# Two feed-forwards in three parts, with the down products in the same list of pairs as the up products and three units of each down pair multiplied by the 7-product scheme

## The reference

```python
h = h + 0.5 * swiglu(rms_norm(h, ffn1_norm), ffn1_w_gate, ffn1_w_up, ffn1_w_down)
...                                  # attention, gated linear attention, merge, w_out
h = h + 0.5 * swiglu(rms_norm(h, ffn2_norm), ffn2_w_gate, ffn2_w_up, ffn2_w_down)
h = h + sigmoid(rms_norm(h, ple_norm) @ w_ple_gate) * (p @ w_ple_proj)
return rms_norm(h, final_norm)
# swiglu(x) = (silu(x @ w_gate) * (x @ w_up)) @ w_down, hidden width 5632
```

## Time and profile before

| | |
|---|---|
| median of 3 runs | 2217.74 us (2217.3 to 2218.07) |
| the profiled execution | 2217.39 us |
| its span, first to last instruction | 2215.3 us |
| PE busy | 2202.3 us, 99% of the span, 9899 matmuls and transposes |
| DVE busy | 1409.5 us, 64% |
| ACT busy | 1073.8 us, 48% |
| DMA | 425.68 MB, 192 GB/s mean |

### The profile page before, as it was taken

The page is one execution under the profiler, slowest core; times in us unless marked ns, Lnnn a source line. Parts: engine busy times, 40 slices in busy tenths (PEclk is TensorE's granted clock), DMA queues, the critical chain, the costliest instruction groups (busy, mean ns, idle before and its releaser), DMA issues.

```text
span 2215.3 us, 24399 instructions
## 1 busy us (share of the span) xinstructions
PE 2202.3 (99%) x9899; PEld 1817.2 (82%) x9899; DVE 1409.5 (64%) x1432; ACT 1073.8 (48%) x1183; POOL 39.4 (2%) x71
## 2 busy tenths in 40 slices
PE   9999999999999999999999999999999999999998
PEld 7888888888888888877777888888888888888886
DVE  5988645688755544445655665788864568875555
ACT  6545443454544444454444545464543346444454
POOL 0000000000010000010010000000000000000000
PEclk9999999999999999999999999999999999999999
DMA  8655555654555666655555665655546665556664
GB/s 288 239 176 193 179 190 186 233 214 173 190 179 187 200 193 195 180 174 169 175 170 161 186 186 180 232 205 180 201 171 190 190 237 200 186 182 198 190 190 143
DMA packets 165705, 425.68 MB, mean 192 GB/s; under 512 B 11592, under 2 KB 11600, under 8 KB 150368
## 3 DMA queue, kind: packets, MB, share of 16 engines
q1 hardware_dynamic: 163840, 419.21, 58.1%
q0 software_dynamic: 1472, 4.70, 0.8%
q10 hardware_dynamic: 288, 0.30, 0.0%
HBM read 422.06 MB, written 2.11 MB: 191 GB/s over the span
## 4 chain that ended last, share of the span: by engine, by line
PE 98%; DMA 1%; issue 0%; DVE 0%; ACT 0%; ACTq 0%; POOLq 0%; POOL 0%
PE acc L1493 18%; PE acc L1495 18%; PE acc L1494 18%; PE acc L1536 6%; PE acc L1538 6%; PE acc L1537 6%; PE turn L1538 4%; PE turn L1536 4%; PE turn L1537 4%; PE fox L1538 4%; PE fox L1537 4%; PE fox L1536 4%; PE turn L1513 1%; DMA raw<-in_ffn_up 0%; PE acc L1530 0%; PE turn L1787 0%
## 5 line engine op out<-in xcount | busy, mean ns | idle before, releaser
L1025 DVE TENSOR_TENSOR w_lo<-raw,w_hi 128x1024 fp32r<-128x1024 f32 x451 | 558.0, 1240 | 585.1 <-ACT w_hi L594 584.6
L594 ACT ACTIVATE w_hi<-raw 128x1024 fp32r<-128x1024 f32 x451 | 477.1, 1060 | 682.9 <-PE acc L1495 643.0
L1493 PE MATMUL acc<-w_hi,x_both 128*128 128x512 f32 x940 | 371.0, 395 | 0.8 <-DVE x_both L1188 0.8
L1495 PE MATMUL acc<-w_hi,x_both 128*128 128x512 f32 x940 | 366.6, 390 | 0.0
L1494 PE MATMUL acc<-w_lo,x_both 128*128 128x512 f32 x940 | 366.3, 390 | 0.0
L1493 PE MATMUL acc<-w_hi,slab_r 128*128 128x512 f32 x832 | 325.5, 391 | 0.0
L1495 PE MATMUL acc<-w_hi,slab_r 128*128 128x512 f32 x832 | 324.2, 390 | 0.0
L1494 PE MATMUL acc<-w_lo,slab_r 128*128 128x512 f32 x832 | 324.0, 389 | 0.0
L1493 PEld LDWEIGHTS acc<-w_hi,x_both 128*128 128x128 f32 x940 | 176.6, 188 | 42.5 <-issue 5.7
L1495 PEld LDWEIGHTS acc<-w_hi,x_both 128*128 128x128 f32 x940 | 176.5, 188 | 37.4
L1494 PEld LDWEIGHTS acc<-w_lo,x_both 128*128 128x128 f32 x940 | 176.7, 188 | 35.2
(11 more groups left out here) (432 smaller groups left out, 3513.6 us busy)
## 6 DMA issues: line engine op xcount, KB each, us to landing
raw<-in_ffn_w_down SPq DMA_DIRECT2D x176, 512.0 KB
raw<-in_ffn_up SPq DMA_DIRECT2D x50, 1024.0 KB, 4.9
raw<-in_w_in SPq DMA_DIRECT2D x96, 512.0 KB
lo_raw<-in_ffn_up SPq DMA_DIRECT2D x42, 1024.0 KB, 4.9
raw<-in_w_merge_gate SPq DMA_DIRECT2D x64, 512.0 KB
more<-in_ffn_up SPq DMA_DIRECT2D x25, 1024.0 KB, 4.9
raw<-in_ffn_up SPq DMA_DIRECT2D x33, 512.0 KB, 3.9
raw<-in_w_out SPq DMA_DIRECT2D x32, 512.0 KB
```

Of the source, the lines that this page charges most:

```text
L594: nc.scalar.activation(w_hi[:, slot, :, :], raw[:, slot, :, :], ACT.Copy).then_inc(hi_split, 1)
L1025: nc.vector.tensor_tensor(w_lo[:, slot, :, :], raw[:, slot, :, :], w_hi[:, slot, :, :].bitcast(F32), ALU.subtract).then_inc(lo_split, 1)
L1493: nc.tensor.matmul(to, hi(kt)[:, tok], w_hi[:, slot, k, :], start=kt == 0, stop=False)
L1495: last = nc.tensor.matmul(to, lo(kt)[:, tok], w_hi[:, slot, k, :], start=False, stop=kt == BK * nb - 1)
```

## The change

The two parts become three (16, 16 and 12 row tiles; 4, 4 and 3 up pairs). The down product of a part becomes two down pairs of 1024 columns each, with 8, 8 and 6 units of two row tiles. Up and down pairs stand in one list of 17 pairs for each ffn and alternate between the bank sets. Every pair but the first (in the first ffn the first two) has three units by the 7-product scheme, down pairs too. Input sums for the down pairs are made from the hidden values, three units for each part: unit 0 in the stage ahead of the part's last up stage, units 1 and 2 in the last up stage. B items are interleaved with S items; `turn_hidden` moves from behind the fifth item to behind the third on PE. The rows of h, p and the inputs of the last phases move to other rooms, and the thin weights of the projection are split later. The core of the diff:

```diff
-HALF_KT = (24, 20)
+PARTS = (4, 4, 3)
-US = 3
+US, HS = 3, 3
+def ffn_pairs():
+    pairs, j = [], 0
+    for part, ups in enumerate(PARTS):
+        kt0 = 4 * sum(PARTS[:part])
+        pairs += [Pair("up", part, j + n, UNITS, 4 * n) for n in range(ups)]
+        pairs += [Pair("down", part, n, 2 * ups, kt0) for n in range(2)]
+        j += ups
+    return pairs
-    own = [("S", pair, u) for u in range(UNITS)]
-    if pair > first:
-        own = [("B", pair, u) for u in range(US)] + own[US:]
-    if pair + 1 < pairs:
-        own = [*own[:-1], *[("A", pair + 1, u) for u in range(US)], own[-1]]
-    return own
+    b, a = shared_units(ffn, i), shared_units(ffn, i + 1)
+    plain = [("S", i, u) for u in range(b, PAIR[i].units)]
+    own = []
+    for u in range(b):
+        own.append(("B", i, u))
+        if len(plain) > 2:
+            own.append(plain.pop(0))
+    own += plain
+    if a:
+        behind = 2 if PAIR[i].units < UNITS else 1
+        own = [*own[:-behind], *[("A", i + 1, u) for u in range(a)], *own[-behind:]]
+    return own
+def turned_at(stage):
+    return 4 if len(stage) >= 10 else 3
```

More of the change, by code:

```diff
@@ L127, in item_tables @@
         slot, at, made = 0, b0, []
-        for p in range(first, pairs):
+        for i in range(first, PAIRS):
             stage = []
-            for kind, pair, u in stage_of(p, first, pairs):
+            for kind, pair, u in stage_of(name, i):
                 q = quads[at - b0]
@@ L164, in filled @@
         n = blk
-        for name in UPS:
-            if blk >= BLOCK[DOWN_OF[name]]:
-                n -= padded(up_items(name))
+        for name, later in NEXT_OF.items():
+            if blk >= BLOCK[later]:
+                n -= padded(ffn_items(name))
         return n // RING + 1
@@ L173, in split_after, with sum_number @@
         return AFTER[first][1][blk % RING // 2] if first in AFTER else blk - RING + 1
[L175 to L178, removed]
+    ADDED = {}
+    for name, first in FIRST.items():
+        for i in range(first, PAIRS):
+            if shared_units(name, i):
+                ADDED[name, i] = len(ADDED) + 1
+    ROWS = {"down1": GROUP["ffn1"] + 2 * (PAIRS - 2), "out": GROUP["out"], "down2": GROUP["ffn2"] + 2 * (PAIRS - 2)}
+    UP_TURN = {"ffn1": TURN["up1"], "ffn2": TURN["up2"]}
     def item_counts(name, it):
-        end = BLOCK[DOWN_OF[name]]
+        end = BLOCK[NEXT_OF[name]]
         return end - it.at if it is STAGES[name][-1][-1] else 1
+    def sum_number(name, pair, u):
+        first = (US + HS * len(PARTS)) * (name == "ffn2")
+        return first + u if PAIR[pair].kind == "up" else first + US + HS * PAIR[pair].part + u
     x_tm = x[0].rearrange("(t p) d -> p t d", p=P)
@@ L1413, in _ @@
                 else:
[L1414 removed]
+                    rows_out(c - 1, start, 1.0)
                 splits(start, 4, 6)
@@ L1538, in product, with plain_part, shared_products @@
                 return nc.tensor.matmul(to, x_rest, w, start=False, stop=stop, skip_group_check=primed)
-            def multiply_item(name, it, hi, lo, primed, last_unit, ready):
+            def plain_part(name, it, ct, hi, lo, primed):
+                banks, whole, rest = banks_of(name, it.pair), hi_quad(name, it.quad), lo_parts(name, it)[0]
+                for k in range(BK):
+                    for t in range(TT):
+                        tok, kt = slice(t * P, (t + 1) * P), BK * it.unit + k
+                        last = product(banks[2 * ct + t][:, :], hi(kt)[:, tok], lo(kt)[:, tok], whole[:, 2 * k + ct, :],
+                                       rest[:, 2 * k + ct, :], not primed and kt == 0,
+                                       not primed and kt == BK * PAIR[it.pair].units - 1, primed)
+                return last
+            def shared_products(name, it, hi, lo):
                 banks, whole = banks_of(name, it.pair), hi_quad(name, it.quad)
@@ L1562, in multiply_item @@
[L1562 to L1567 removed]
+                sum_hi, sum_lo = sums_of(it.pair, it.unit)
@@ L1569, in tiles_of, with feed_forward @@
+                for n, (x, x_rest, bank) in enumerate(of_tokens):
+                    last = product(banks[bank][:, :], x, x_rest, whole[:, n, :], rest[n], begin, end, it.kind == "B")
+                return last
             def tiles_of(first_turn):
                 return lambda j: pe.wait_ge(turned_lo, first_turn + j + 1)
-            def up_groups(name, hi, lo, sums=None, first_rows=None):
-                pairs, first = UPS[name]
+            hidden_of = of(slab_r, slab_r, 0, HID)
+            def feed_forward(name, x_pair, first_rows=None, p_turn=False):
+                down_turn = "down" + name[-1]
```

515 lines of the change are left out of this document (249 added, 266 removed).

## The result

The changed kernel takes 2238.26 us (median of 4 runs, 2238.05 to 2239.2) against 2217.52 (4 runs, 2217.14 to 2218.07) for the kernel before: ratio 1.0093, 95% interval 1.0079 to 1.0106. It is slower, as forecast, but by 20.7 us where I had said 7.5, and it lies above my range. Its profiled execution has a span of 2237.5 us, 22.2 more than before.

A forecast was written before the change was run, and what follows sets the result against it. PE's count of matmuls was taken to bound the kernel. Savings of 28.6 us against added waits of 11.4, 18.0 and 6.65 us gave +7.5 us, so 2225 us, with a range of 2209 to 2236.

The forecast's parts named there:

- twelve waits for the sums: Last up stage of each part and the stage ahead: input sums delay A1's split, 0.95 us each, 11.4 us.
- the long one of the short stage: First down stage of the last part: trio load, steps A1, then A0's split; PE stands still 5.9 us.
- the ones of the last stages: Last down stage: PE waits 2.65 us for splits; in the second ffn 0.9 and 3.1 us; sum 6.65 us.
- PE's 126 matmuls: Up and down pairs: 14 more pairs share units, saving 9 matmuls each at 0.227 us, 28.6 us off PE.
- the short stages: First down stage of each ffn's last part: waits ahead of B2, A0 and A1, 9.0 us per ffn, 18 us.
- the 2.1 us wait that I had forecast: Short down stage, ahead of A1: DVE gives an A each 4.86 us, PE takes 2.72, so PE waits 2.1 us.
- the first of my two figures: Short down stage: low clock for A0's 12 matmuls costs 0.6 us; through all three A items, 6.1 us a stage.
- the sum: Whole kernel: -28.6 + 11.4 + 18.0 + 6.65 = +7.5 us, 2225 us; other added work put at nothing.
- starts of both ffn: Beginning of each ffn: the prediction had no term for waits there, 0 us.
- Other stages lose their 1.7 us too: Rival: seven more stages that follow an up pair wait, 1.5 us each, giving 2235 us; chance 0.08.
- The price of a wait: Stages with input sums: a wait costs PE's idle until the split, 0.9 us, 0.95 with the handover.
- The wait of 5.9 us in the short stage is the first inside the kernel that could do this: Short down stage: the granted clock could fall to half behind this wait; rival with it low through A items, 2232, chance 0.15.

The follow-up runs named there:

- raw-space: Changed kernel with raw spaces 0, 1, 4, 0 for the second ffn's first four items, in place of 0, 1, 0, 1: 2235.03 us.
- plain-pair: Changed kernel with the last down pair of each ffn multiplied plainly, 9791 matmuls instead of 9773: 2230.05 us.
- The run with PE kept busy: Changed kernel with 75 matmuls whose results nobody reads filling PE's long waits: 2236.21 us.
- the short stage reordered: Changed kernel with the short down stage as B0 B1 B2 S3 S4 A0 A1 A2 S5: 2228.72 us.
- the sums moved: Changed kernel with ten of twelve input-sum places moved in DVE's and ACT's lists, out of the stretch ahead of the A items: 2224.44 us.
- The kernel of three edits: Changed kernel with each ffn's last down pair plain, raw spaces 0, 1, 4, 0 at the second ffn's start, and ten input sums moved: 2212.53 us.
- the list alone: Changed kernel with no down pair shared and no sums for them, raw and high-part spaces set at the starts: 2218.19 us.

## Why the prediction was right and wrong

**Right.** The sign, and the mechanism of every wait in three of the four groups: twelve waits for the sums (forecast 0.95 us, seen 0.95 to 0.99); the long one of the short stage (5.9; 5.62 and 5.41), through trio load, steps, then A0's split; the ones of the last stages (2.65 and 0.9; 2.67 and 0.98). The second ffn's was 2.72 and not 3.1. PE's 126 matmuls are 28.6 us as said. The clock fell behind both waits of the short stages (0.51 and 0.54 granted behind 5.62 and 5.41 us). By the rule of the Trainium skill that the prediction cites, "TensorE: Matmul & The Clock Gate", "Why this matters for your kernels", it should, and there the trace agrees. But it stayed low for A0 alone, where it took the place of the 2.1 us wait that I had forecast (2.4 and 2.0 us lost), the first of my two figures. That the short stages come to 18.1 us where I had said 18.0 is therefore luck in part: 4.2 us of forecast waits did not come, and 4.4 us of slow matmuls stood in their place.

**Wrong, in size**, by 13.9 us (21.4 accounted, 7.5 forecast). By the terms of the sum:

| term | forecast | measured |
|---|---|---|
| 126 matmuls | -28.6 | -28.6 |
| sums, 12 waits | +11.4 | 11.6 idle + 3.2 = +14.9 |
| short stages | +18.0 | 12.6 idle + 1.1 + 4.4 slow clock = +18.1 |
| last stages | +6.65 | 6.4 idle + 0.8 + 2.9 slow clock = +10.1 |
| starts of both ffn | 0 | 3.5 idle + 0.5 + 2.9 slow clock = +6.9 |

1. The step that failed most is "the sum", where other waits were put at nothing. Both starts were missing in it: the number of loads in a ffn sets which raw space the first ones get, and the change alters that number. None of my rivals had it ("Other stages lose their 1.7 us too" names others, and those did not wait). For the second ffn the raw-space and plain-pair runs show the cause, from both sides; for the first (0.68 us) it is read from the list and the trace alone.
2. The price of a wait. I priced PE's standing still at the time until the split is there, 0.95 with 0.05 for the handover. A stage with one takes 1.26 us longer, and over 21 waits the 0.27 that I left out are 5.7 us. The chain gave me the distance of matmul starts, and there was no wait in it from which to read that price; the earlier trace rows had three, and I did not measure around them.
3. The clock. "The wait of 5.9 us in the short stage is the first inside the kernel that could do this" was wrong: in the changed kernel it fell behind 2.80 and 2.72 us too, and there it came on top of the idle, 2.9 us each. The run with PE kept busy gave back all of it in the last stage and 1.6 us at the start. The earlier trace rows only showed that it falls some time after the last matmul.

## What to carry to other kernels

When an engine without slack is given less work, price each new wait at its idle plus what stopping and starting costs, and ask whether the clock falls behind it and what would hide that. When a change alters the number of items in a list, work out every rotation of buffers that counts from an end of it, at both ends. And work saved on PE by added work on DVE is worth its place in DVE's list: the same 126 matmuls cost 21 us or bring 9, by where sums, B items and loads stand.

## What was not expected of the hardware

Over eleven kernels with waits of PE, behind the first 25 us: matmuls started 0.43 us apart behind each of the twelve waits of 3.5 us and longer, at once or up to five matmuls later (behind the 3.78 us of the plain pair the first four distances were at full speed). Behind waits of 2.65 to 3.13 us this was so 12 times of 17, with no difference at the place that I could find: 2.67 us at the same item had no slow matmul in the changed kernel and seven or eight with the short stage reordered or the sums moved; 2.72 us at another had 15 in the changed kernel and none with the short stage reordered. The number of slow matmuls varied as well, 6 to 15. Behind 1.66 us and less it never happened; behind two of 1.83 us once. In the first 25 us three kernels had one wait each, of 2.10, 2.27 and 2.60 us, with five to seven distances of 0.43 us behind it, so waits shorter than 2.65 us can have it too. The kernel of three edits, with two waits of 2.8 us, spread by 6.1 us over ten runs, the list alone, with none above 1.2 us there, by 2.3 over ten; that fits, and shows no more than that. What decides it, for waits of one length, was not tried and stays open.
